# Query projection from the raw turned residual, with the norm as a row at the reads

## The reference

```python
x = x + gate1[:, None, :] * y                      # y = merged @ w_out
h2 = modulate(rms_norm_2(x, norm2_w[l]), shift2, scale2)   # norm(x) * w * (1 + scale2) + shift2
...
q = jnp.einsum('btd,dq->btq', h, w_q).reshape(B, T, H, 2, PEER_DQ // 2)    # 1024 -> 2048
s1 = jnp.einsum('bthc,kc->bthk', q[..., 0, :], keys1)      # scores against 128 keys, twice
...                                                 # top 16 of each, of their sums, softmax g
a = gelu(einsum('pd,ped->pe', xx, expert_down[ii]))
y2 = einsum('pe,ped->pd', gg * a, expert_up[ii])
...
x = x + gate2[:, None, :] * y2
return rms_norm_2(x, final_norm_w)
```

## Time and profile before

| | |
|---|---|
| median of 3 runs | 1415.91 us (1415.56 to 1416.72) |
| profiled execution, its own time | 1417.08 us |
| its span, first to last instruction | 1415.3 us |
| mean granted TensorE clock | 0.988 |
| busy: TensorE, GpSimd, VectorE, ScalarE | 1371.8, 1055.6, 757.9, 710.4 us |
| DMA | 263.02 MB, mean 186 GB/s |

### The profile page before, as it was taken

How to read it: one execution, slowest core, us unless ns; L and a number is a source line. 1 busy time by engine, 2 the same in 40 slices (tenths; PEclk the granted TensorE clock), 3 DMA queues, 4 the chain that set the end, 5 groups by cost and what they waited for, 6 DMA issues and landing times.

```text
span 1415.3 us, 28961 instructions
## 1 busy us (share of the span) xinstructions
PE 1371.8 (97%) x9764; PEld 1220.6 (86%) x9764; DVE 757.9 (54%) x1617; ACT 710.4 (50%) x1133; POOL 1055.6 (75%) x469
## 2 busy tenths in 40 slices
PE   7998999999999998999999999999999999999997
PEld 7887899998877876999999999999977777878885
DVE  4655433335258526249991276666588788511113
ACT  6354555555355444435556533433455555556663
POOL 6654688886777985768888877777777777788885
PEclk9999999998999999999999999999999999999999
DMA  8453677763645456545555544444445444465552
GB/s 306 153 179 120 237 282 275 284 256 134 208 144 175 159 185 250 191 132 187 180 183 186 179 164 157 154 162 155 156 159 166 164 163 163 168 248 193 193 193 89
DMA packets 72651, 263.02 MB, mean 186 GB/s; under 512 B 8208, under 2 KB 9104, under 8 KB 72224
## 3 DMA queue, kind: packets, MB, share of 16 engines
q1 hardware_dynamic: 72608, 262.46, 53.9%
HBM read 259.81 MB, written 2.62 MB: 185 GB/s over the span
## 4 chain that ended last, share of the span: by engine, by line
PE 88%; DVE 6%; issue 2%; ACT 1%; DMA 1%; POOL 1%; SPq 0%; ACTq 0%; POOLq 0%; DVEq 0%
PE bank L865 14%; PE bank L883 14%; PE bank L866 14%; PE bank L867 14%; PE bank L884 13%; PE bank L885 13%; PE bank L1271 3%; DVE arena L1741 1%; POOL wlo L433 1%; DMA raw<-stream 1%; PE bank L983 1%; PE bank L1253 1%; DMA col<-cols 0%; PE bank L941 0%; DVE bank L1369 0%
## 5 line engine op out<-in xcount | busy, mean ns | idle before, releaser
L433 POOL TENSOR_TENSOR wlo<-raw,whi 128x1024 fp32r<-128x1024 f32 x432 | 1041.6, 2423 | 320.1 <-ACT whi L503 316.9
L503 ACT ACTIVATE whi<-raw 128x1024 fp32r<-128x1024 f32 x432 | 455.8, 1057 | 347.4 <-PE bank L885 256.9
L865 PE MATMUL bank<-xh,whi 128*128 128x256 f32 x1600 | 462.4, 289 | 4.2 <-DVE xl L1332 2.4
L866 PE MATMUL bank<-xl,whi 128*128 128x256 f32 x1600 | 455.4, 285 | 0.0
L867 PE MATMUL bank<-xh,wlo 128*128 128x256 f32 x1600 | 455.0, 284 | 0.0
L883 PE MATMUL bank<-whi,xh 128*128 128x512 f32 x800 | 321.6, 402 | 12.0 <-DVE xl L1939 4.1
L865 PEld LDWEIGHTS bank<-xh,whi 128*128 128x128 f32 x1600 | 309.8, 194 | 9.4 <-POOL wlo L433 3.7
L884 PE MATMUL bank<-wlo,xh 128*128 128x512 f32 x800 | 313.1, 391 | 0.0
L885 PE MATMUL bank<-whi,xl 128*128 128x512 f32 x800 | 312.9, 391 | 0.0
L866 PEld LDWEIGHTS bank<-xl,whi 128*128 128x128 f32 x1600 | 309.9, 194 | 1.2
L867 PEld LDWEIGHTS bank<-xh,wlo 128*128 128x128 f32 x1600 | 309.6, 193 | 0.0
(11 more groups left out here) (285 smaller groups left out, 1160.3 us busy)
## 6 DMA issues: line engine op xcount, KB each, us to landing
raw<-stream SPq DMA_DIRECT2D x432, 512.0 KB, 3.3
arena<-ada SPq DMA_DIRECT2D x48, 512.0 KB, 4.8
arena<-rows SPq DMA_DIRECT2D x5, 512.0 KB, 8.6
xs<-x SPq DMA_DIRECT2D x2, 512.0 KB, 6.0
arena<-rows SPq DMA_DIRECT2D x1, 1024.0 KB, 5.5
x_spill<-xs SPq DMA_DIRECT2D x1, 1024.0 KB, 6.1
xs<-x_spill SPq DMA_DIRECT2D x1, 1024.0 KB, 6.1
out<-arena SPq DMA_DIRECT2D x2, 512.0 KB, 2.6
```

Source lines behind the costliest of these rows:

```text
L433: nc.gpsimd.tensor_tensor(wlo[:, slot, :], raw[:, slot, :], whi[:, slot, :].bitcast(F32), ALU.subtract).then_inc(lo_done, 1)
L503: nc.scalar.activation(whi[:, slot, :], raw[:, slot, :], ACT.Copy).then_inc(hi_done, 1)
L865: nc.tensor.matmul(dst, h_, xh[:, k, :], start=(k == 0), stop=False)
L866: nc.tensor.matmul(dst, h_, xl[:, k, :], start=False, stop=False)
```

## The change

The query matmuls no longer wait for the norm.

- TensorE turns `xres` itself, into banks 4, 5, 7 and 0 (`turn_of`): the first token half ahead of the second half of the last `wout2` tile, the second half piece by piece as x3 is added. `upper_raw` and `turned_raw` split the turned values times the gain.
- `xh` and `xl` become views of `xhs` and `xls`, whose chunks have 258 columns; the two extra columns hold the shift. The 16 query tiles stream 258 columns into banks 1 and 2, so that columns 256 and 257 are W times shift.
- The inverse root is turned into a row (`root_row`, two transposes in bank 3) after the second query tile. VectorE's read of a query tile becomes three operations (`normed`): copy the shift column, multiply by the row, add the column.
- The experts still want normed, shifted values: VectorE multiplies the turned banks by gain and row (`rowed`, behind the reads of tiles 2 to 5), ScalarE adds the shift (`shifted`), and they are split a second time into `xh` and `xl` (`upper_normed`, `turned_normed`), two banks under the second half of the last query tile, two after it.
- The last two `ada` tiles move behind the lower split; the two gate rows behind query tile 3 (rows in banks 6 and 3) and their additions behind the read of tile 6. The key scores use banks 1, 2, 3 and 6. In SP's queue the keys' load moves ahead, the spill of the residual and of `gate2` behind the issue of query weight tile 15. GpSimd makes one root of both halves after the split of weight tile 3.
- In the tail the last four expert tiles run over two banks at a time.

```diff
-        xh = sb("xh", [P, KC, T], F32R)
-        xl = sb("xl", [P, KC, T], F32R)
+        xhs = sb("xhs", [P, KC, T + 2], F32R)
+        xls = sb("xls", [P, KC, T + 2], F32R)
+        xh, xl = xhs[:, :, 0:T], xls[:, :, 0:T]
...
+        wq_r = go[:, 0, 0:T]
...
@@ SP @@
-            for n in range(T_WQ, T_WQ + 8):
+            for n in range(T_WQ, T_WQ + 16):
...
                 if n == T_WQ + 2:
+                    sp.dma_start(ky.rearrange("p a b -> p (a b)"), keys).then_inc(S("keys_in"), 16)
...
-            sp.wait_ge(S("unturned"), scaled_at("wq", 2))
+            sp.wait_ge(S("turned_lo"), turn("wq", 4, 4))
+            sp.wait_ge(S("squares"), squared("wq"))
             sp.dma_start(x_spill, xs[:, :]).then_inc(S("spilled"), 16)
...
@@ GpSimd @@
-            los(T_IN2_M + 40 + R - 1, T_WQ + 1)
-            root(S("squares"), squared("wq", 1), s_(SS["n2"])[:, 0:1], rs("n2", 0), 1.0 / D)
-            lo((T_WQ + 1) % R, T_WQ + 2)
-            root(S("squares"), squared("wq", 2), s_(SS["n2"])[:, 1:2], rs("n2", 1), 1.0 / D)
-            pool.wait_ge(S("unturned"), scaled_at("wq", 2))
-            los(T_WQ + 2, T_END)
+            los(T_IN2_M + 40 + R - 1, T_WQ + R)
+            root(S("squares"), squared("wq"), s_(SS["n2"]), rs("n2"), 1.0 / D)
+            los(T_WQ + R, T_END)
...
@@ ScalarE @@
+            def shifted(n, group, shifts):
+                for b in range(4):
+                    act.wait_ge(S("rowed"), n + b + 1)
+                    for j in range(2):
+                        src = bank[turn_bank(group, b)][:, j * T:(j + 1) * T]
+                        own(nc.scalar.activation(src, src, ACT.Identity, bias=shifts[:, 2 * b + j:2 * b + j + 1]))
+            def upper_raw(group, gains, shifts):
+                nc.scalar.activation(xhs[:, :, T:T + 2], shifts.unsqueeze(2).to_broadcast([P, KC, 2]), ACT.Copy)\
+                    .then_inc(S("shift_hi"), 1)
+                for b in range(4):
+                    act.wait_ge(acc_ready, acc_filled(group, b))
+                    for j in range(2):
+                        k = 2 * b + j
+                        last = nc.scalar.activation(xh[:, k, :], bank[turn_bank(group, b)][:, j * T:(j + 1) * T], ACT.Copy,
+                                                    scale=gains[:, k:k + 1])
                     last.then_inc(S("turned_hi"), 1)
...
-            upper_of(T_WQ + 1, T_WQ + 2)
-            act.wait_ge(S("roots"), rooted("wq0"))
-            act.wait_ge(S("squares"), squared("wq", 1))
-            nc.scalar.activation(xn[:, 0, :], xres[:, 0, :], ACT.Copy, scale=rs("n2", 0)).then_inc(S("unturned"), 1)
+            upper_of(T_WQ + 1, T_WQ + R)
+            act.wait_ge(S("gain_set"), 2)
+            upper_raw("wq_T", gain[:, 8:16], mod[:, 16:24])
             act.wait_ge(S("x3_done"), 4)
             sums(xres[:, 1, :], 1, D, xn, s_(SS["n2"]), S("squares"))
-            upper_of(T_WQ + 2, T_WQ + R)
-            act.wait_ge(S("gain_set"), 2)
-            upper_shifted("wq_T", gain[:, 8:16], mod[:, 16:24], 2)
-            his(T_WQ + R, T_PEER + R)
+            his(T_WQ + R, T_WQ + 2 * R + 2)
+            shifted(0, "wq_T", mod[:, 16:24])
+            his(T_WQ + 2 * R + 2, T_PEER + R - 1)
+            act.wait_ge(S("wq_half"), 1)
+            upper_normed("wq_T", (0, 1))
+            act.wait_ge(tile_used, T_PEER)
+            upper_normed("wq_T", (2, 3))
+            upper_of(T_PEER + R - 1, T_PEER + R)
...
@@ TensorE @@
-            m_group_by_halves(T_WOUT2, "wout2", 3, "merged")
+            m_group_by_halves(T_WOUT2, "wout2", 3, "merged",
+                              before_last=lambda: turn_of("wq_T", xres, "x3_done", 0, range(4)))
+            turn_of("wq_T", xres, "x3_done", 1, range(4))
...
+            query_tile(0, "wq")
+            query_tile(1)
+            pe.wait_ge(S("roots"), rooted("wq"))
+            root_row("n2", bank[3], "wq_row")
+            query_tile(2)
+            query_tile(3)
+            pe.wait_ge(S("wq_row_out"), 1)
             for g in (10, 11):
                 ada_row(g)
...
-            for b in range(4):
+            for banks in ((0, 1), (2, 3)):
                 for c in range(N_PEER - R, N_PEER):
-                    expert_m(c, None, final=(c == N_PEER - 1), banks=(b,), used=b == 3)
+                    expert_m(c, None, final=(c == N_PEER - 1), banks=banks, used=banks == (2, 3))
...
@@ VectorE @@
+            def rowed(group, gains, row, b):
+                for j in range(2):
+                    k = 2 * b + j
+                    src = bank[turn_bank(group, b)][:, j * T:(j + 1) * T]
+                    last = stt(src, src, gains[:, k:k + 1], row, ALU.mult, ALU.mult)
+                last.then_inc(S("rowed"), 1)
+            def normed(n, d_, src, row, scale, done):
+                if n >= 2:
+                    v.wait_ge(S(done), n - 1)
+                wshift = wshifts[:, n % 2:n % 2 + 1]
+                own(nc.vector.tensor_copy(wshift, src[:, T:T + 1]))
+                own(ttt(d_, src[:, 0:T], row, ALU.mult)); own.sync()
+                if scale is None:
+                    tsc(d_, d_, wshift, None, ALU.add).then_inc(S(done), 1)
...
-                if b == 2:
-                    for n in range(N_ADA - 2, N_ADA):
-                        ada_tile(n)
...
-            v.wait_ge(S("roots"), rooted("wq1"))
-            tsc(xn[:, 1, :], xres[:, 1, :], rs("n2", 1), None, ALU.mult).then_inc(S("unturned"), 1)
             v.wait_ge(S("gain_set"), 2)
-            turned_shifted("wq_T", "wq", gain[:, 8:16], mod[:, 16:24])
-            for g in (10, 11):
-                gate_row(g, gate2, "gate2_b").then_inc(S("gate2_done"), 1)
-            chunks(T_WQ, 16, pq, 0, S("pq_out"))
+            shift_lower(SHIFTS["wq"], mod[:, 16:24])
+            turned_raw("wq", gain[:, 8:16])
+            for n in range(N_ADA - 2, N_ADA):
+                ada_tile(n)
+            v.wait_ge(S("wq_row"), 1)
+            nc.vector.tensor_copy(wq_r, bank[3][:, 0:T]).then_inc(S("wq_row_out"), 1)
+            v.wait_ge(S("wq_row_out"), 1)
+            for n in range(N_WQ):
+                v.wait_ge(tile_used, T_WQ + n + 1)
+                normed(n, pq[:, n, :], bank[1 + n % 2], wq_r, None, "pq_out")
+                if 2 <= n < 6:
+                    rowed("wq_T", gain[:, 8:16], wq_r, n - 2)
+                if n == 6:
+                    for g in (10, 11):
+                        gate_row(g, gate2, "gate2_b").then_inc(S("gate2_done"), 1)
+            turned_normed("wq_T", "wqn")

```

More of the change, by code:

```diff
@@ L67, in acc_freed @@
         return "go_done", 1
+    if group == "wq_T":
+        return (("turned_lo", turn("merged", 4, 1)), ("turned_lo", turn("merged", 4, 2)),
+                ("turned_lo", turn("merged", 4, 4)), ("x3_done", 1))[bank]
     if group == "in2_T":
@@ L856, in _, with f_tile @@
         def _(pe):
-            def f_tile(slot, count, dst, turned=None):
+            def f_tile(slot, count, dst, turned=None, xh=xh, xl=xl, half=None):
                 pe.wait_ge(lo_done, count)
@@ L867, in f_tile @@
                     last = nc.tensor.matmul(dst, l_, xh[:, k, :], start=False, stop=(k == KC - 1))
+                    if half and k == KC // 2 - 1:
+                        last.then_inc(S(half), 1)
                 last.then_inc(tile_used, 1)
@@ L1017, in ada_row @@
                 pe.wait_ge(ada_used, 4 * (g - g % 2 + 2))
-                nc.tensor.matmul(bank[6 + g % 2][:, :], one.to_broadcast([P, P]), ada_sum(g), start=True, stop=True)\
+                nc.tensor.matmul(bank[ROW_BANK[g]][:, :], one.to_broadcast([P, P]), ada_sum(g), start=True, stop=True)\
                     .then_inc(S("ada_rows"), 1)
@@ L1252, in _ @@
                     tt, m = n // 16, n % 16
-                    last = nc.tensor.matmul(bank[q % 4][:, j * P:(j + 1) * P], pq[:, m, tt * P:(tt + 1) * P],
+                    last = nc.tensor.matmul(bank[SCORE_BANKS[q % 4]][:, j * P:(j + 1) * P], pq[:, m, tt * P:(tt + 1) * P],
                                             ky[:, m % 2, :], start=True, stop=True)
@@ L1261, in expert_f @@
                     pe.wait_ge(S("expert_act"), k + (c - 1))
-                f_tile(c % R, k + (T_PEER + c + 1), bank[4 + c % 2][:, 0:T])
+                f_tile(c % R, k + (T_PEER + c + 1), bank[4 + c % 2][:, 0:T], "wqn" if i is None and c == 0 else None)
             def weights4(q, i):
@@ L1380, in gate_row @@
                 dst = gate[:, (g % 2) * 512:(g % 2 + 1) * 512]
-                return ttt(dst, bank[6 + g % 2][:, :], dst, ALU.add)
+                return ttt(dst, bank[ROW_BANK[g]][:, :], dst, ALU.add)
             def filled(group, b, tiles_end):
```

94 lines of the change are left out of this document (68 added, 26 removed).

## The result

The changed kernel takes **1424.08 us** (median of 5 runs, 1422.76 to 1426.29), the kernel before 1416.67 beside it on the same chip (1415.56 to 1416.94): ratio **1.0055, 95% interval 1.004 to 1.0069**, slower. The forecast was 1412.4, range 1411.0 to 1415.2. The profiled execution after took 1426.29 us, its span 1424.5 (before: 1417.08 and 1415.3), at a mean granted clock of 0.986 (before 0.988).

The account below looks back on a forecast made before the run. TensorE's chain (88% of the span) was taken as the bound, with idle waits in the seam before the query. Seam 3.1 plus tail 0.5, less 0.1 for semaphores: 1415.9-3.5=1412.4 us, range 1411.0 to 1415.2.

Parts of the forecast that it names:

- The structure of the seam: Between output projection and key scores: raw values split early, new waits and gate rows on the path; 3.1 us saved.
- the first query matmul: After the output projection: it starts at about 564.9 instead of 570.76, 5.9 us earlier.
- the row wait: Before query tile 2: TensorE idles 1.6 to 1.7 us until VectorE has copied the root row and read tile 0.
- the gate rows: Behind query tile 3: two rows moved from an idle seam into TensorE's full stream, costing 1.82 us.
- one of the named signs: In the seam: the forecast is wrong if ScalarE starts the upper split later than 563.1.
- The tail: Last four expert tiles over two banks at a time: 0.5 us saved, between 0 and 0.6.
- VectorE, free at 563.65 plus the shift's lower part, agrees: Before the first query matmul: VectorE, done with x3 and the shift's lower split, also allows the start at 564.95.
- add 0.35: In VectorE's read of query tile 0, ahead of tile 2: adding the shift column takes 0.35 us.
- The clock: In the seam: full clock expected after a 3.3 us pause; rival, it falls, costing 1.8 us, 1414.2 us, chance 0.20.
- the same pitch of 0.120 in the experts: In the experts' matmuls of 256 columns: the pitch stays 0.120 us despite the new layout.
- a rival at 0.06: Matmuls of 256 columns: uneven 1,032-byte rows cost one more reading step, 1417.0 or 1421.5 us; chance 0.06.
- 258 columns: In the query tiles: two more columns on each of 384 matmuls cost 0.3 us.

Follow-up runs that it names:

- e4: The changed kernel with the query read's product kept in PSUM and the shift columns split ahead of the x3 reads: 1416.46 us (1.0006).
- e2: The kernel before with xh and xl as 256 used columns in rows of 258, nothing else: 1419.67 us (1.0026).
- e9: The changed kernel with only the split of the shift columns moved ahead of the x3 reads: 1421.18 us (1.004).
- e1: The kernel before, unchanged, run once more as a control: 1415.74 us (1.0003).
- e7: The kernel before with 128 unused bytes per partition ahead of xh and xl: 1421.76 us (1.0036).
- e8: The kernel before with 64 unused bytes between xh and xl: 1421.49 us (1.0045).
- e13: The kernel before with xh and xl in rows of 260 columns, 256 used: 1412.03 us (0.9974).
- e11: The changed kernel with both stalling VectorE operations cured, rows of 260 and the two gate rows moved into the wait ahead of query tile 2: 1408.58 us (0.9948).

## Why the prediction was wrong, step by step

**The structure of the seam was right.** Taking the stalls away (e4), the first query matmul starts 3.65 us after the output projection, forecast 3.75; the row wait is 1.57, forecast 1.6 to 1.7; the gate rows 1.88 in a full stream, forecast 1.82; no half clock, as forecast. ScalarE's side, one of the named signs, was right too: in the changed kernel the copy of the shift columns took 0.20 us and the eight uppers 3.02, as forecast. Counted from the same point (0.85 us of transposes now lie ahead of the last half tile), e4's key scores come 59.27-55.08-0.85 = 3.3 us sooner, 2.8 against e2, which has the same pitches; forecast 3.1. The tail gives 0.4 to 0.5, forecast 0.5. e4 against e2, the whole change on one layout and without the stalls, is 3.2 us by the medians and 2.8 by the ratios; forecast 3.5.

**The step that failed first** is the price of two short VectorE operations: "VectorE, free at 563.65 plus the shift's lower part, agrees", and in the root row's chain "add 0.35". Both were priced as if alone. They took 1.95 and 2.48 us, because each began during a GpSimd subtraction. The most that any case of mine allowed for an operation of the read was 0.5 us, and for the shift's lower part nothing was set apart. With the clock falling twice behind the longer pauses they cost 6.9 us in all (changed kernel against e4 by the ratios, and by the seams, 62.01 and 55.08; 7.6 by the medians). Such a stall had its row in the trace before, the 128x8 product of 2.06 us; I sized operations by elements and didn't ask which engine was busy beside them.

**The clock** was given 0.20 for one fall, as a matter of the pause's length. It fell twice. Part of that follows from the stalls, but not all: in five kernels with a first pause of 3.65 us it stayed full, in e9 with the same pause it fell. The length of that pause alone doesn't decide it.

**The second step that failed** is one that the forecast took for granted: "the same pitch of 0.120 in the experts", and 0.227 for the wide matmuls, in a kernel with another layout. It put this at nothing; e2 shows 3.7 us (1.0026, 1.0016 to 1.0036). The layout was a rival at 0.06, as one more reading step for uneven rows of 256-column matmuls. That mechanism is wrong: those matmuls became quicker, by some 0.0011 us each, and rows of 260 and 264 (all even) move the pitch too. What I didn't have at all is the wide matmuls, with the tokens as the stationary side, which became slower by 0.0042. By the pitches, 4,800 x -0.0011 and 2,784 x 0.0042 give some +6 us, an estimate; e2 measured +3.7, and its profiled execution has 6.8 us less at half clock ahead of the seam than e1's. So that rival was right in that the layout makes the kernel slower, and by luck: its mechanism would have slowed the matmuls that became quicker. The reason the forecast gave against it was no better, since it held a duration (284 ns) against a pitch (7.38/64 = 0.115 us).

**258 columns** were put at 0.3 us; with rows of 258 they are 384 x (0.1202-0.1188) = 0.5, with rows of 260 384 x (0.1213-0.1175) = 1.5.

The sum, by the ratios: +3.7 (layout, e2) - 2.8 (the change itself, e4 against e2) + 6.9 (stalls and clock, the changed kernel against e4) = +7.8 us, which is the changed kernel's 1.0055. It must come out, since each term is the difference of two neighbours in one chain of kernels. It says how the loss is split, and doesn't test the causes; those rest on the rows and pitches above.

Open: by which mechanism the relative place of the operands sets the pitch, what besides the pause decides whether the clock falls, and how much of the 6.9 us is the pauses themselves and how much the clock.

## What to carry to other kernels

Price a short VectorE operation by its operands and by what GpSimd does beside it: with all inputs in SBUF it could cost here a whole GpSimd instruction, with a PSUM input it didn't, so leave an intermediate in PSUM or do it in idle time. A changed row length or a new buffer moves every tensor behind it, and that alone made this kernel up to 6 us slower (e7, e8) or 4 us faster (e13); before judging an edit, run the old code with the new layout. Fill a wait on TensorE with work that is due anyway, as e11 did, and look for a layout last.

## What the runs showed of the hardware

- A VectorE subtraction of 16 columns took 1.95 to 2.30 us and an addition over 256 columns up to 2.48 us (2.00, 1.52 and 1.03 in the last tiles of the query) beside GpSimd's subtraction of 2.34 us; from PSUM the same addition took 0.48 us. Eight additions of 256 to 32 columns, all in SBUF, took 10.22 us beside it and 1.33 with GpSimd idle.
- The pitch of fp32r matmuls at full clock was between 0.1175 and 0.1200 us for 256 columns and between 0.2271 and 0.2333 for 512, by the place of tokens to weights in SBUF and the row length: unchanged by a common move of 128 bytes or a move of the tokens by 6,144, changed by one of 128. The two kinds don't go together: rows of 260 are best for the narrow, the old layout for the wide.
- With the same 3.65 us pause the clock stayed at 2.4 GHz in five kernels and fell to 1.2 GHz in one. The stretch at 1.2 GHz at 151 to 158 us was there in one profiled execution of the kernel before and not in the other.
